# One threshold of the fill order in a 16-pair recurrent stage: the first group of turned keys of direction 1 goes ahead of the mask wait

## The reference

```
def step(s, inp):
    r_t, w_t, k_t, v_t, a_t, b_t = inp
    sa = jnp.einsum('bhvk,bhk->bhv', s, a_t)
    s = s * w_t[:, :, None, :] + sa[..., None] * b_t[:, :, None, :] + v_t[..., None] * k_t[:, :, None, :]
    return s, jnp.einsum('bhvk,bhk->bhv', s, r_t)
s_last, ys = lax.scan(step, s0, xs, reverse=reverse)
...
yn = merge_heads((y - mean) * lax.rsqrt(var + RWKV_GN_EPS))
return ((yn + merge_heads(bonus)) * jax.nn.silu(gate.astype(jnp.float32))).astype(dtype)
```

## Time and profile before

| | us |
|---|---|
| median of three runs | 2558.18 |
| the three runs | 2558.18, 2558.61, 2554.99 |
| the profiled execution | 2554.59 |
| span in it, first to last instruction | 2552.8 |
| PE busy in it | 2477.2 (97%) |
| DVE, ACT, POOL busy | 1180.5, 764.5, 417.4 |
| mean granted clock of TensorE | 0.988 of full |

### The profile page before, as it was taken

How to read it: one execution, slowest core, us unless ns; L and a number is a source line. 1 busy time by engine, 2 the same in 40 slices (tenths; PEclk the granted TensorE clock), 3 DMA queues, 4 the chain that set the end, 5 groups by cost and what they waited for, 6 DMA issues and landing times.

```text
span 2552.8 us, 62193 instructions
## 1 busy us (share of the span) xinstructions
PE 2477.2 (97%) x27332; PEld 1653.1 (65%) x27332; DVE 1180.5 (46%) x2455; ACT 764.5 (30%) x1526; POOL 417.4 (16%) x446
## 2 busy tenths in 40 slices
PE   5999999999999998899999999999999999999998
PEld 1566676666666676668888854446544468775787
DVE  4766666666666664453663333305611114442412
ACT  3444444545445443131221310004400014102301
POOL 2443433344443441000011000000000000000000
PEclk8999999999999998899999999999999999999999
DMA  6211111111111104634447532210234434431343
GB/s 247 95 38 46 38 46 46 39 38 38 48 38 39 46 20 168 221 128 149 132 132 278 199 107 74 75 66 29 78 132 140 132 130 141 132 124 62 95 155 101
DMA packets 80131, 258.08 MB, mean 101 GB/s; under 512 B 11639, under 2 KB 16984, under 8 KB 79096
## 3 DMA queue, kind: packets, MB, share of 16 engines
q1 hardware_dynamic: 75304, 242.94, 28.4%
q0 software_dynamic: 1360, 5.89, 0.6%
q10 hardware_dynamic: 3200, 5.27, 0.6%
HBM read 253.02 MB, written 1.05 MB: 100 GB/s over the span
## 4 chain that ended last, share of the span: by engine, by line
PE 57%; DVE 1%; DMA 1%; ACT 0%; issue 0%; DVEq 0%; SPq 0%; ACTq 0%
PE ps L1962 13%; PE ps L2130 10%; PE ps L1907 9%; PE ps L1832 7%; PE ps L2147 5%; PE ps L1992 4%; PE ps L2034 2%; PE ps L1761 1%; PE ps L2054 1%; PE ps L2019 1%; PE ps L2074 1%; PE ps L2013 1%; PE ps L1940 1%; PE ps L1928 1%; PE ps L1893 1%; DMA ring<-in_w_mods 1%
## 5 line engine op out<-in xcount | busy, mean ns | idle before, releaser
L1962 PE MATMUL ps<-h,ring 128*128 128x256 f32 (+1 forms) x1184 | 358.9, 465 | 0.0
L1962 PEld LDWEIGHTS ps<-h,ring 128*128 128x128 f32 x1184 | 225.0, 190 | 132.6 <-issue 114.3
L2130 PE MATMUL ps<-h,ring 128*128 128x512 f32 (+1 forms) x768 | 256.1, 486 | 0.0
L1907 PE MATMUL ps<-h,ring 128*128 128x256 f32 x1024 | 225.6, 379 | 0.0
L1907 PEld LDWEIGHTS ps<-h,ring 128*128 128x128 f32 x1024 | 193.9, 190 | 34.9 <-issue 9.9
L2130 PEld LDWEIGHTS ps<-h,ring 128*128 128x128 f32 x768 | 145.0, 190 | 101.7 <-issue 91.8
L1033 ACT ACTIVATE general<-general 64x512 f32<-64x512 f32 x160 | 101.8, 636 | 161.7 <-DVE general L1232 159.1
L561 PE MATMUL ps<-general,ring 128*128 128x512 f32 x256 | 134.9, 623 | 0.8 <-issue 0.8
L577 PE MATMUL ps<-general,ring 128*128 128x512 f32 x256 | 134.1, 629 | 0.0
L2147 PE MATMUL ps<-general,ring 128*128 128x512 f32 (+1 forms) x384 | 131.0, 486 | 0.0
L752 PEld LDWEIGHTS ps<-general 64*64 64x64 f32 (+1 forms) x5120 | 78.2, 131 | 71.8 <-issue 48.1
(11 more groups left out here) (373 smaller groups left out, 4089.7 us busy)
## 6 DMA issues: line engine op xcount, KB each, us to landing
ring<-in_w_mods SPq DMA_DIRECT2D x96, 512.0 KB, 5.5
ring<-in_w_feature SPq DMA_DIRECT2D x74, 512.0 KB, 3.5
ring<-in_w_rkvg SPq DMA_DIRECT2D x64, 512.0 KB, 3.7
ring<-in_w_in SPq DMA_DIRECT2D x48, 512.0 KB, 3.5
ring<-in_w_merge SPq DMA_DIRECT2D x48, 512.0 KB, 3.4
ring<-in_w_out SPq DMA_DIRECT2D x32, 512.0 KB, 6.3
ring<-in_w_token SPq DMA_DIRECT2D x24, 512.0 KB, 3.7
ring<-in_w_merge SPq DMA_DIRECT2D x48, 256.0 KB, 3.0
```

The lines of the kernel that those rows point to most:

```text
L1907: mm = pe.matmul(ps[:, n % 4, 0:NX], weights(key, k), R.h[:, k, 0:NX], start=(k == 0), stop=(k == KD - 1))
L1962: mm = pe.matmul(ps[:, feature_bank(l, j), 0:width], weights(("feature", l, j), k), R.h[:, k, cols], start=(k == 0), stop=(k == KD - 1))
L2130: mm = pe.matmul(ps[:, 2 * b, 0:NQ], weights(key, k), R.h[:, k, 0:NQ], start=(k == 0), stop=(k == KD - 1))
```

## The change

```
-FILL_MASKS = 500
+FILL_MASKS = 700
```

## The result

The changed kernel takes 2560.57 us in the median of 20 runs, the kernel before 2556.36 us in the median of 20 on the same chips: +4.2 us, a ratio of 1.0018 with a 95% interval of 1.0012 to 1.0025. So it is a little slower, by an amount that lies just inside the 0.2% bound of the forecast; the interval reaches past it. The predicted 2560.6 us was on the point by luck: it stood on the median of the first three runs of the kernel before, 2558.18, which later runs moved down by 1.8 us. The forecast difference was +2.4 us, the measured one +4.2.

A forecast was written before the change was run, and what follows sets the result against it. PE's own work was taken to set the pace in pairs 0 to 14. +0.24 us a pair over 14 pairs (+3.4) and -1.0 in pair 15 gave +2.4 us, so 2560.6 us, range 2552 to 2572.

The forecast's parts named there:

- The moved group: Four transposes ahead of the mask wait would wait for ACT's copy L1023, so below(1) starts 0.54 us later.
- it fits: Faster rival: the moved group fits the 0.6 us hole before below(1), with squares in time; 2549.6 us, chance 0.14.
- `turn_out`: Standing earlier behind turn_reads, it would find POOL's normalise ready: 0 us, bounds 0 and 0.75.
- `norm`: Standing earlier behind below(3), it would wait 0.26 us for POOL's squares; bounds 0 and 0.4.
- The end of the pair: Four gate pieces move ahead of advance 1 (+1.71 us); advance 1 to first_blocks falls from 7.55 to 5.90 us (-1.65).
- Sum of an inner pair: All terms of pairs 1 to 14 together: +0.24 us a pair, +3.4 us over 14 pairs.
- Pair 15: turn_out and bonus_weights would stand where PE idles 0.98 us ahead of grow(2): -1.0 us.
- The clock rival: Longer idle times bring 4 us of each pair to granted clock 0.69: +17 us, 2578 us, chance 0.04.

The follow-up runs named there:

- the kernel with the moved group alone: Kernel before with only the four transposes moved ahead of the mask wait, order unchanged from grow(1) on: 2557.45 us, 1.0009 of the kernel before.
- Gates behind: The kernel with the steps filled, with the last two gate pieces moved from the last two step gaps to behind read_states: 2559.7 us, 1.0009 of the kernel before.
- gates ahead: Kernel before with the two gate pieces behind read_states moved ahead of advance 1: 2565.22 us, 1.0029 of the kernel before.
- the kernel with the steps filled: Changed kernel with two fewer gate pieces ahead of advance 1 and one in each of the six chunk step gaps: 2557.25 us, 1.0004 of the kernel before.

## Why the prediction was right, and where not

*The moved group: right.* Priced at +0.54 us with the hole kept; `below(1)` came 0.55 us later, with L614 waiting 0.41 us for L1023 (0.6 was forecast). The alternative "it fits" died on ACT's row, and the kernel with the moved group alone confirmed it.

*`turn_out`: right, on the finest margin.* The sum had POOL's `normalise` over just as DVE's scan begins. In the changed kernel POOL

```profile
405.45 0.61 POOL L1457 TENSOR_TENSOR x<-x,general 128x256 f32<-128x256 f32 x1 [1.86 <-ACT general L1069]
```

ends at 406.06, and DVE starts the scan at

```profile
406.04 1.22 DVE L1146 TENSOR_TENSOR_SCAN sq<-rstd,h 128x512 f32<-128x512 f32 x1
```

The instruction fell from 1.36 us to 0.61 in all inner pairs, L633 doesn't wait, and 0.75 us a pair, or 10.5 us, did not appear. The Trainium skill, "SBUF — State Buffer", section "SBUF: two separate sides", on the port pair that VectorE and GpSimd share, says that the one that starts first holds the pair for its whole instruction and the other blocks; for a VectorE operation with two SBUF inputs this holds against a GpSimd one that reads SBUF. The rows agree in kind: POOL begun first takes 0.61 us, begun 0.25 us behind the scan it takes 1.36, and the masks that read PSUM don't slow it. In degree they don't quite: the slow one ends 0.40 us behind the scan, less than its own 0.61 us, so some of its time passed beside the scan.

*`norm`: right.* Priced at +0.26, measured 0.23 in 14 pairs.

*The end of the pair: right in kind, 0.18 us too small.* I priced `advance` 1 to `first_blocks` at 5.90 us; it is 6.08. The term that was too small is the PE work of `advance` 6, taken as 0.42 us: from L855 at 443.90 to L865 at 444.48 it is 0.58, and `read_states` then takes 0.84. In a filled step L855 does take 0.42 us up to the gate piece behind it (440.54 from 440.12 in the trace); why it takes longer here was not tested. The wait at `advance` 6 was 0.25 us (0.4 was forecast).

*Sum of an inner pair:* forecast +0.24, measured +0.34 to +0.43 (pairs of 57.88 and 57.97 us; 57.8 was forecast). Most of the rest lies in that term.

*The holes: missing.* The step that fell short is the first paragraph's claim that "only two things can change the time: PE's waits, and how well its pieces pack". A third could, and it was in the rows' trace: holes without a releaser, with an excess of 3.2 us over pairs 1 to 14 in the kernel before. In the changed kernel they are some 3 us more. Gates behind and gates ahead show which order raises them, and the instruction transfers what ends them. I treated the two gate pieces behind `read_states` as plain cost, to be moved at par.

*Pair 15: too small.* Forecast -1.0 us, measured -3.6 and, in the second profiles, 76.2 to 71.9, -4.4. The mask wait there is 0.4 us (0.9 in the second profile) where it was 1.5, and the mean granted clock over the pair is 0.88 and 0.91 in the two profiles in place of 0.82 in both. PE's busy time fell by 3.1 and 2.9 us, which is most of the gain, so the clock is the larger part of it and the waits the smaller. The forecast counted only the 0.98 us ahead of `grow(2)`. That the group fills the mask wait of this one pair, which has no `low` and so no ACT chain ahead of the copy, was in the trace and not in the sum. That the clock follows from the shorter waits is a guess that was not tested by itself; the holes of this pair, 6 to 9 us in every profile, move too.

Together: 14 x 0.4 + 3 - 4 is about +5 us, measured +4.2 in the medians. The forecast of +2.4 was right to 2 us because two terms of about 3 us that it lacked have opposite signs. That is luck, not foresight.

*The clock rival* is out: inner pairs run at a granted clock of 1.00 with the group next to an idle stretch (pair 6 of the changed kernel):

```profile
445.32:504.24 58.92, 57.34 (x1341) 39.93 (x1338) 37.26 (x75) 28.06 (x55) 22.80 (x24) 1.00 0.13 40
```

So the caution drawn from the Trainium skill's "PE-mode transpose" section ("TensorE: Matmul & The Clock Gate") costs nothing here.

## What to carry to other kernels

A hole in front of a wait is not filled by work that itself waits for an engine whose result is due at the same moment: of the candidates for the gap, take the one whose inputs are oldest (here a key piece, -10.7 us with the packing that came along, against a group of transposes, no gain). A budget that moves one piece moves all behind it, so count the whole period, and judge each moved piece by the slack at its new place. Wide matmuls between blocks of many small ones do more than their own work: taking them from there cost 8 us and 4 to 6 us on two bases, though each pair by itself got shorter. Where they could go into free gaps instead, as in the kernel with the steps filled, gain and loss came out even. And where PE idles for no shown reason, look at the instruction queue's transfers.

## What the runs showed of the hardware

PE can stand still in the middle of an unblocked series of small float32 matmuls, 0.2 to 2.5 us at a time in the inner pairs. How often depends on the order: putting two gate pieces (four wide matmuls) between `read_states` and `first_blocks` took the excess of pairs 1 to 14 from 10.8 to 1.8 us, taking them away raised it from 3.2 or 6.0 to 17.2 us, with all work kept. What PE waits for is its instructions: of 130 such stretches in twelve profiles 129 end 1.2 to 1.7 us behind the end of a 16-KB transfer on the instruction queue. That a dense run of small instructions uses them up faster than they come fits this; what sets the time of a transfer was not tested.

Behind one idle stretch of 1.68 us the granted clock fell to its lower level for some 3.4 us; behind the other holes of the inner pairs it did not, one of 2.5 us among them.

A chunk step of matmul, copy and back takes 0.87 us without a gate piece of 0.43 us in it, and 0.88 to 1.09 us with one, so pieces in the six gaps of a pair are all but free. A seventh has no such gap.
